# The output stages of two feed-forward layers: where the seven-product blocks stand among the ordinary units, and when their shared sums are made

## The reference

```
first block:   x = x + rms_norm((silu(gate) * up) @ w_ffn_out, ffn_post_g)
second block:  h = h + (silu(a) * b) @ ffn_w_out            then the final rmsnorm
```

## Time and profile before

| what | us |
|---|---|
| median of three runs (2441.11 to 2443.13) | 2441.84 |
| the profiled execution | 2439.61 |
| its span, first to last instruction | 2437.3 |
| TensorE matmuls busy (share of the span) | 2402.9 (99%) |
| TensorE weight loads busy | 1999.5 (82%) |
| VectorE busy | 1774.3 (73%) |
| ScalarE busy | 1336.0 (55%) |
| mean granted clock of TensorE | 0.999 of full speed |

### The profile page before, as it was taken

One profiled execution on the slowest core, in us unless ns is written; L12 is line 12 of the kernel. 1 busy time (PEld: TensorE's weight loads), 2 busy tenths in 40 slices (PEclk: granted clock), 3 DMA queues, 4 the chain that ended last, 5 costly groups with the idle time before them and its releaser, 6 DMA issues.

```text
span 2437.3 us, 33576 instructions
## 1 busy us (share of the span) xinstructions
PE 2402.9 (99%) x12147; PEld 1999.5 (82%) x12147; DVE 1774.3 (73%) x2434; ACT 1336.0 (55%) x1853; POOL 36.9 (2%) x60
## 2 busy tenths in 40 slices
PE   9999999999999999999999999999999999999998
PEld 7888888887788888887887889898788888887776
DVE  5568888677888878886666436677788888887565
ACT  5665558666555555554445436564655555555453
POOL 1000000000000000000000010000000000000000
PEclk9999999999999999999999999999999999999999
DMA  7766545445556565656566774435565556655554
GB/s 232 243 208 187 162 150 176 158 166 171 178 193 206 189 200 187 204 199 205 170 224 199 214 228 154 134 114 164 164 207 184 196 189 196 214 192 194 186 190 155
DMA packets 233854, 455.83 MB, mean 187 GB/s; under 512 B 16698, under 2 KB 19002, under 8 KB 233232
## 3 DMA queue, kind: packets, MB, share of 16 engines
q1 hardware_dynamic: 227008, 431.49, 54.9%
q0 software_dynamic: 6160, 21.81, 2.6%
q10 hardware_dynamic: 576, 1.05, 0.1%
HBM read 449.04 MB, written 5.24 MB: 186 GB/s over the span
## 4 chain that ended last, share of the span: by engine, by line
PE 87%; DVE 6%; DMA 4%; ACT 2%; issue 1%; SPq 0%; DVEq 0%; ACTq 0%
PE g L1275 12%; PE g L1277 12%; PE g L1276 12%; PE g L348 6%; PE g L350 5%; PE g L349 5%; PE g L1749 4%; PE g L1750 4%; PE g L1751 4%; DVE wl L336 2%; PE m L1130 2%; PE m L1132 2%; PE m L1131 2%; DMA raw<-in_ffn_w_out 2%; DMA raw<-in_w_ffn_out 1%; PE g L2686 1%
## 5 line engine op out<-in xcount | busy, mean ns | idle before, releaser
L336 DVE TENSOR_TENSOR wl<-raw,wh 128x1024 fp32r<-128x1024 f32 (+1 forms) x820 | 988.2, 1219 | 488.3 <-ACT wh L332 473.3
L332 ACT ACTIVATE wh<-raw 128x1024 fp32r<-128x1024 f32 (+1 forms) x819 | 858.2, 1055 | 822.4 <-PE g L1277 290.0
L1275 PE MATMUL g<-wh,act_hi 128*128 128x512 f32 x960 | 374.9, 391 | 0.0
L1277 PE MATMUL g<-wh,act_lo 128*128 128x512 f32 x960 | 373.6, 389 | 0.0
L1276 PE MATMUL g<-wl,act_hi 128*128 128x512 f32 x960 | 373.5, 389 | 0.0
L1275 PE MATMUL g<-wh,ht_hi 128*128 128x512 f32 x544 | 213.2, 392 | 6.3 <-DVE wl L336 6.3
L1276 PE MATMUL g<-wl,ht_hi 128*128 128x512 f32 x544 | 212.4, 390 | 0.0
L1277 PE MATMUL g<-wh,ht_lo 128*128 128x512 f32 x544 | 212.4, 390 | 0.0
L1275 PEld LDWEIGHTS g<-wh,act_hi 128*128 128x128 f32 x960 | 180.2, 188 | 38.5 <-issue 0.7
L1277 PEld LDWEIGHTS g<-wh,act_lo 128*128 128x128 f32 x960 | 180.2, 188 | 37.6
L1276 PEld LDWEIGHTS g<-wl,act_hi 128*128 128x128 f32 x960 | 180.2, 188 | 37.1
(11 more groups left out here) (517 smaller groups left out, 3885.0 us busy)
## 6 DMA issues: line engine op xcount, KB each, us to landing
raw<-in_w_ffn_in SPq DMA_DIRECT2D x176, 512.0 KB, 4.5
raw<-in_ffn_w_in SPq DMA_DIRECT2D x176, 512.0 KB, 4.5
raw<-in_w_in SPq DMA_DIRECT2D x111, 512.0 KB, 4.5
raw<-in_w_ffn_out SPq DMA_DIRECT2D x88, 512.0 KB, 4.8
raw<-in_ffn_w_out SPq DMA_DIRECT2D x88, 512.0 KB, 4.6
raw<-in_nsa_w_in SPq DMA_DIRECT2D x80, 512.0 KB, 4.1
raw<-in_w_out SPq DMA_DIRECT2D x32, 512.0 KB, 4.2
raw<-in_nsa_w_out SPq DMA_DIRECT2D x32, 512.0 KB, 4.6
```

What stands on the lines that cost most here:

```text
L332: nc.scalar.activation(wh[:, j % SLOTS, 0:n], raw[:, j % SLOTS, 0:n], ACT.Copy).then_inc(hi_done, 1)
L336: nc.vector.tensor_tensor(wl[:, j % SLOTS, 0:n], raw[:, j % SLOTS, 0:n], wh[:, j % SLOTS, 0:n].bitcast(F32), ALU.subtract).then_inc(lo_don ...
L1275: nc.tensor.matmul(dst, h, whk, start=(t in starts and k == 0), stop=False)
L1277: ins = nc.tensor.matmul(dst, l, whk, start=False, stop=(last and k == 1))
```

## The change

The list is built by another rule. A pair's gaps are now pairs of numbers: before the first block 6 units of the even chunk; before the second 6 of the even one; before the third 4 of the even and 3 of the odd; before the fourth 1 and 6; behind it 1 and 9. Both pairs have the same gaps. The first block stands at places 6 and 58 (before: 9 and 57), the others 10 or 11 places apart; before it was 6 or 7 places within the first pair and 7 or 8 in the second. The even chunk ends at places 42 and 94 (before: 33 and 85), the odd one at 51 and 103 as before. `OUT_OPEN` holds the place of a chunk's first unit, since chunks now overlap.

The shared sums, all six operations behind place 6 counted from the fourth block's start, are dealt out: the first at 7, the second at 8, the third and fourth at 9, the additions into `x` of the second layer at 8 and 10. The other work at fixed places (n = 2 to 7) stays at its numbers. Steps `up` and `gate` change numbers, since they are now made in the other order. Numbers of instructions, of matmuls and of loads are the same.

```diff
-FO_GAPS = ((9, 3, 2, 2, 2), (5, 4, 3, 3, 3))
+FO_GAPS = ((6, 0), (6, 0), (4, 3), (1, 6), (1, 9))
...
-    for p, gaps in enumerate(FO_GAPS):
-        units = list(range(FO_K, FKT // 2))
-        left = iter(units)
-        for b, gap in enumerate(gaps):
-            order += [("unit", 2 * p, next(left), 0) for _ in range(gap)]
+    for p in range(2):
+        left = [iter(range(FO_K, FKT // 2)) for _ in range(2)]
+        for b, gap in enumerate(FO_GAPS):
+            for c, n in enumerate(gap):
+                order += [("unit", 2 * p + c, next(left[c]), 0) for _ in range(n)]
             if b < FO_K:
                 order += [("seven", p, b, q) for q in range(4)]
-        order += [("unit", 2 * p + 1, u, 0) for u in units]
...
+OUT_OPEN = [min(n for n, o in enumerate(OUT) if o[0] == "unit" and o[1] == c) for c in range(4)]
...
-                    opens = n == 0 or OUT_END[c - 1] == n - 1
+                    opens = n == OUT_OPEN[c]
...
-            def up_rows(p):
-
+            def shared_2(p):
                 dve.wait_ge(ff_kept, fo_m1_kept(name, p))
                 dve.wait_ge(unit_used, SLOTS + s["u0"] + OUT_AT[FO_K * p + FO_K - 1] + 4)
                 nc.vector.tensor_tensor(fo_step[:, :], kept[:, 0, :], m[:, 3, :], ALU.add).then_inc(ff_step, 1)
+
+            def shared_3(p):
                 dve.wait_ge(ff_step, fo_stepped(name, p, FO_STEP["u2"]))
                 nc.vector.tensor_tensor(kept[:, 1, :], fo_step[:, :], m[:, 1, :], ALU.add).then_inc(ff_step, 1)
                 dve.wait_ge(ff_step, fo_stepped(name, p, FO_STEP["u3"]))
+
+            def shared_rest(p):
                 nc.vector.tensor_tensor(rest[p][:, 0, :], fo_step[:, :], m[:, 2, :], ALU.add)
                 nc.vector.tensor_tensor(rest[p][:, 1, :], kept[:, 1, :], m[:, 2, :], ALU.add).then_inc(ff_step, 1)
...
-                if n - 6 in OUT_AT and OUT[n - 6][2] == FO_K - 1:
-                    p = OUT[n - 6][1]
-                    up_rows(p)
-                    if name == "fo2":
-                        for c in range(2):
-                            rows_into(p, c, x[:, :, (2 * p + c) * NB:(2 * p + c + 1) * NB])
+                for p in range(2):
+                    since = n - OUT_AT[FO_K * p + FO_K - 1]
+                    if since == 7:
+                        shared_2(p)
+                    if since == 8:
+                        shared_3(p)
+                    if since == 8 and name == "fo2":
+                        rows_into(p, 0, x[:, :, 2 * p * NB:(2 * p + 1) * NB])
+                    if n == OUT_END[2 * p] + 4 and name == "fo1":
+                        dve.wait_ge(unit_used, used(s, 2 * p))
+                        rows_into(p, 0, g[:, 0:T, :])
+                    if since == 9:
+                        shared_rest(p)
+                    if since == 10 and name == "fo2":
+                        rows_into(p, 1, x[:, :, (2 * p + 1) * NB:(2 * p + 2) * NB])
```

More of the change, by code:

```diff
@@ L1053, in build @@
         FO_STEPS = 2 * (FO_K + 6)
-        FO_STEP = {"t2": 1, "u2": FO_K + 1, "u3": FO_K + 2, "up": FO_K + 3, "gate": FO_K + 4, "rest": FO_K + 5}
+        FO_STEP = {"t2": 1, "u2": FO_K + 1, "u3": FO_K + 2, "gate": FO_K + 3, "up": FO_K + 4, "rest": FO_K + 5}
         STEPS = {"t2": (1, 3), "rows": 2, "u2": 4, "u34": 5, "shared": 6}
@@ L1384, in dve_out @@
                     dve.wait_ge(ff_summed, summed_no(name, b + 1))
-                if n - 6 in OUT_AT and OUT[n - 6][2] == FO_K - 1:
-                    p = OUT[n - 6][1]
-                    up_rows(p)
-                    if name == "fo2":
-                        for c in range(2):
-                            rows_into(p, c, x[:, :, (2 * p + c) * NB:(2 * p + c + 1) * NB])
+                for p in range(2):
[13 more added lines that the diff above has]
+                        rows_into(p, 1, x[:, :, (2 * p + 1) * NB:(2 * p + 2) * NB])
+                if n == OUT_END[1] + 4 and name == "fo1":
+                    dve.wait_ge(unit_used, used(s, 1))
+                    rows_into(0, 1, g[:, T:2 * T, :])
                 for chunk in range(3):
[L1392 to L1395, removed]
                     if n == OUT_END[chunk] + (5 if name == "fo1" else 4):
-                        evac(p, c)
+                        evac(chunk // 2, chunk % 2)
         def pe_ffn_in(pe, name, turn):
```

## The result

| | us |
|---|---|
| median of four runs (2424.34 to 2426.07) | 2425.03 |
| the kernel before beside it, median of four (2438.64 to 2443.13) | 2441.48 |
| ratio, 95% interval | 0.9934 [0.9918, 0.9949] |
| the profiled execution, and its span | 2426.07, 2423.8 |

The account below looks back on a forecast made before the run. TensorE, busy 99% of the span, was taken as the bound, so only its waits could give time back. 17.2 us removed less 5.6 added gave 11.6 us less: 2430 us against a median of 2441.84, range 2425 to 2434.

Parts of the forecast that it names:

- Waits ahead of blocks and behind the sums: Both output stages: all go, 4.2 and 5.1 us ahead of blocks; behind the sums 0.5 and 6.0, plus 1.4 half clock.
- gaps of two: Blocks two units apart: weights come 1.4 us too late, and the four such blocks lost 1.3 to 1.7 us.
- the longest load: Weight load ahead of a block: even the longest shown, 5.78 us, leaves 1.4 us with gaps of six or seven.
- The half clock of the kernel before: Second stage, behind the 3.53 us wait at 2379.10: half speed for 3.00 us, costing 1.4 us, which the change removes.
- The opening: First block of each stage, moved from place 9 to 6: new waits of 0.4 and 2.4 us, 5.6 us in both stages.
- The walk of VectorE's queue: First block of each stage: VectorE's work followed step by step from place 5, giving 2.8 us of new waiting.
- Rival 2: Openings of both stages: the bunched waits cost half clock too, 2 x 1.4 us more, 2433 us; chance 15%.
- The shared sums: Behind each pair's last block: dealt out in portions of at most 3.2 us, hidden by VectorE's 5.8 us lead.
- rival 1: Openings of both stages: they cost little, up to 1 us, so the time is 2425 us; chance 12%.
- rival 3: Second stage's shared sums: portions still show, 1 to 2 us lost at each of two places, 2433 us; chance 8%.
- rival 4: At the 16 blocks: mixed units make ScalarE or VectorE later, slower than before, 2448 us at 2.0 us late; chance 2%.
- rival 5: Ahead of blocks: waits only move, 9.3 us stay because loads are slower than 5.8 us, 2439.5 us; chance 6%.

Follow-up runs that it names:

- sums_later: The changed kernel with the second sums of activations and their low part moved from places 6 and 7 to 12 and 13: 2418.01 us, ratio 0.9905.
- before_a: The kernel before, without an edit, for a second profile: 2438.26 us, ratio 0.9997.
- nine_first: The changed kernel with its first pair's first block back at place 9, gaps of 9, 5, 6, 6 and 10 units: 2416.17 us, ratio 0.9909.
- deal_only: The changed kernel with the old order of units and blocks, keeping the shared sums dealt out: 2432.79 us, ratio 0.9963.
- order_only: The kernel before with only the new order of units and blocks, shared sums still in one piece: 2424.94 us, ratio 0.9935.
- plain_later: order_only with the sums of activations at places 3, 4, 12 and 13: 2418.32 us, ratio 0.9898.
- gaps_three: sums_later with three units between blocks and the first block at place 8: 2432.19 us, ratio 0.9978 to the kernel before.

## Why the prediction came out as it did

**A kernel without losses as the measure.** The two stages of sums_later have neither a wait nor a fall of the clock: 234.8 + 234.4 = 469.2 us. What a profile has above that is what its stages lose. The kernel before: 20.0 us in the first profile, 24.4 in before_a. The changed kernel: 9.0. The prediction had priced 17.2 and 5.6.

**Waits ahead of blocks and behind the sums.** Their places, their number and that they all go were right. Their size was not, in two ways. First, one execution was taken for all: 15.7 us of waits in the first profile, 6.4 + 12.6 = 19.0 in before_a. By the medians too the first profile was mild: the kernel before lies 22.2 us above nine_first in group 2 and 23.7 above sums_later in group 1. Second, the prices missed 2.8 us in the prediction's own trace. The matmul behind the first one after a wait starts about 0.1 us late as well (1102.53 to 1102.84, not 0.227), 1.2 us for eleven waits; a fall costs 1.6 us and not 1.4; the rest, about 1.4 us, is in waits too short for the profile's list. The prediction said that gaps of two lost 1.3 to 1.7 us; in deal_only's trace they lose up to 2.3, with the load 0.75 us longer. It took 5.78 us for the longest load; the same trace has one of 6.47 in its chain (at 2351.88).

**The half clock of the kernel before.** One fall was counted, 1.4 us. before_a has two, 3.2 us.

**The opening.** Forecast 0.4 + 2.4 = 2.8 us of waiting in each stage. Measured idle times of 0.21 and 2.04, with 0.16 each 0.37 + 2.20 = 2.6; the first stage of order_only, with these waits and no fall, is 3.0 us longer than that of sums_later. The walk of VectorE's queue was right step by step, and sums_later shows the cause.

**Rival 2**, half clock behind the openings, came true in both stages, at 15%. The forecast had the clock unchanged and was wrong there by 2 x 1.6 us, against the other miss in sign. The rule that the prediction cited from the Trainium skill's page "TensorE: Matmul & The Clock Gate" pointed to it: two waits close together did what one wait of 2.49 us had not done. But nearness alone does not decide it: in order_only the same two waits left the clock alone in the first stage, and in deal_only the fall came behind single waits of 1.8 us of idle time.

**Account.** Between before_a and the changed kernel the stages lose 24.4 - 9.0 = 15.4 us less. Waits with 0.16 each make 18.9 - 5.2 = 13.7 of it, late matmuls behind them about 1.0, waits too short for the list about 0.8; the falls cancel, two in either kernel. But for rounding that is the whole. Between the medians it is 16.5 to 16.8 us; where the last 1.1 to 1.4 us are is open.

**How much of it was luck.** The forecast missed by 5 us, and the median is inside the range by 0.03 us; in group 1 the changed kernel took 2424.92. Two misses of opposite sign met: more was removed than was priced, and the new falls of the clock gave 3.2 us of it back. Had the clock stood, as forecast, the time would have been near 2422 us (an estimate), outside the range.

**The shared sums.** That portions of 3.2 us are hidden was right. That the dealing out is what hides them was argued, and is wrong: order_only has one piece of 5.35 us at the same place and loses nothing that its time shows. The price that the prediction put on this step (6.0 + 1.4 us) belongs to the gaps in this kernel; in deal_only, alone, it belongs to the dealing out.

**Rivals 1, 3, 4 and 5** did not happen. The time lies at the edge where rival 1 had put it (2425), for another reason.

## What to carry to other kernels

Read waits that hang on a DMA from more than one profile before they are priced: here the same kernel lost 20.0 us in two stages in one execution and 24.4 in the next. A kernel whose stage has no wait at all is the best measure of what the others lose in it. When a block is moved to an earlier place, list what the busy engine does between the old place and the new one; whatever stays at its old number lands in the middle of the block. Two cures for one wait do not add: measure each alone before both are kept.

## What had not been expected of the hardware

- The kernel before runs at medians of 2438.3, 2441.7 and 2443.4 us in the three groups, while sums_later, nine_first and plain_later, with next to no waits for loads in the two stages, stay at 2416.2 to 2418.3. That the scatter between chips or groups sits in the waits for DMA would fit; it is not shown.
- Loads of 512 KB took 4.8 us in one chain and 5.6 at the same place in another; behind a fourth block 5.5 in one profile and 6.9 in the next, of the same kernel.
- With equal waits of 0.2 and 2.0 us of idle time the granted clock fell to half in five openings of six (both of the changed kernel in two profiles, one of two in order_only). Among single waits it fell behind two of 1.8 us in deal_only and one of 3.0 in before_a, and not behind one of 2.3 in the first profile. In gaps_three twelve waits of up to 1.3 us brought no fall. What decides it is open.
